# A two-layer encoder with 32 experts per layer: sums kept in PSUM, the gather reading x, one more weight buffer

## The chip, the cores and the metric

The kernel runs on one core of one Trainium2 chip. The metric is the device time of one execution in microseconds. It is written in Bass: every engine has its own instruction list, and semaphores tie them together.

## The reference, cut to what matters

Two layers on x of 256 tokens by 1024 floats, all fp32. The part that the change touches is the second half of a layer:

```
h = rms_norm(x, norm2_g)
g = h @ w_rg + b_rg ; grp = argmax(g)            # 4 groups
e = h @ w_re + b_re, within grp                  # 8 experts a group
gate = softmax(g)[grp] * softmax(top2(e))
for each token and each of its 2 experts:
    y = (silu(h @ w_gate[e]) * (h @ w_up[e])) @ w_down[e]     # 1024 -> 512 -> 1024
    x += gate * y
```

Before it stands the mixer half: a projection by w_in (1024 x 2304), three kinds of attention, a projection by w_out. All 32 experts' weights, 6 MB each, are read in every layer.

## The kernel before

**Staging.** Weights flow through pieces of 1 MB (128 partitions by 2048 floats). Sixteen form the ring; six more, `beside`, are lent by arrays that are idle during the experts: two and the early one in `work`, `tables`, `biased`, `hT`. `ring_plan` (lines 102 to 140) walks through all weights of both layers in the order of use and gives each the piece that comes free first, and with it the semaphore count that SyncE waits for before it issues the load (`piece_in`, line 447). `BESIDE_FREE` says at which count each lent piece is free. Items 8 to 10 use the ring alone, as the next mixers need the arrays. `HALVED` names three pieces a layer that are loaded as two halves, the first half already at half a round (`p_half`). All loads go through SyncE's one queue, in order.

**Items.** The experts are done in 11 items a layer. Items hold 1, 2 or 4 experts, with 128, 64 or 32 token places each, side by side in the 128 columns of TensorE (in order of time 2, 2, 4, 1, 4, 1, 4, 2, 4, 4, 4 experts). An item is: the choice (`pick`, a 0/1 matrix of tokens by places, and `pickw`, the same times the gate weight), built on VectorE from seat numbers (`picks`, line 1714; for item 0 line 1699); the gather, TensorE products with `pick` as the moving operand and the normalised rows as the stationary one (`gathers`, line 948), copied to `xg` by VectorE and ScalarE with the gain of the norm; six rounds (`round_of`, line 978: gate0, gate1, up0, up1, down0, down1, each over one piece of every expert of the item); the transposes of `pickw` (line 1039) and of `hid` (line 1057, read with a step of 4 floats); and `back` (line 1012), four products that scatter y to the tokens. VectorE then adds the four banks to x (line 1750) in each item. The gather of item i+1 is done inside item i, its lower half after round 3 and its upper half after the transposes of `hid`.

**Banks.** Of the eight PSUM banks, 0 and 1 take the gather, 2 the gate product, 3 the up product, 4 and 5 the transposes, 6 and 7 the down product, and 2 to 5 the four products of `back`, so TensorE waits for VectorE's additions (`v_back`) before it writes to 2 to 5 again.

**The normalised rows.** `normed_rows` (line 1207) on ScalarE writes x times the norm's factor into `h`, regrouped so that each block of 128 columns is contiguous; the source is read with a step of 8 floats. The squares before it (line 1125) use `h` as a place to dump.

**The last item** of a layer has matmuls without use between its rounds (`warm`), the turning of the next layer's gains and biases, and its down product in parts, so that little is left behind the last landing.

**Reruns** handle an expert that has more tokens than places. No instruction of that part is in the trace.

## Time and profile before

| what | value |
|---|---|
| median of 3 runs | 1176.21 us (1175.89 to 1178.5) |
| the profiled execution | 1178.81 us, its span 1177.0 us |
| TensorE matmul busy | 997.6 us (85%) |
| VectorE busy | 327.1 us (28%) |
| ScalarE busy | 170.9 us (15%) |
| DMA | 436.80 MB, mean 371 GB/s over the span |
| mean granted TensorE clock | 0.939 |

Busy shares are means over very different stages: the mixers run from the start to about 144 us and from about 585 to 727 us, the experts fill the rest. Matmuls are pipelined, so a busy TensorE is not one at its peak. The DMA share is that of the core's 16 DMA engines; at 1.0 they have no gap.

### The profile page before, as it was taken

The page shows a single profiled execution, that of the slowest core. Times are in us where ns is not written, and L with a number is a line of the kernel's source. Part 1 is how long each engine was busy: PE and PEld are TensorE (multiplying, and loading weights), DVE is VectorE, ACT ScalarE, POOL GpSimd, SP SyncE. Part 2 cuts the span into 40 slices and gives each one's busy share as a digit, 9 for nine tenths or more (in the row PEclk, how much of TensorE's full clock was granted, in tenths as well). Part 3 has the DMA queues.
Part 4 walks back from the last instruction along what each step waited for, and adds up shares of the span by engine and source line. Part 5 has one row for each costly group of instructions (what it writes and reads, how often), then busy time and mean ns, then how long its engine had stood idle before and what let it go on. Part 6 is the DMA issues. An engine that isn't in the chain of part 4 may idle for free.

```text
span 1177.0 us, 14082 instructions
## 1 busy us (share of the span) xinstructions
PE 997.6 (85%) x5406; PEld 467.7 (40%) x5406; DVE 327.1 (28%) x742; ACT 170.9 (15%) x440; POOL 51.6 (4%) x104
## 2 busy tenths in 40 slices
PE   8999999998977946659899999999969779474686
PEld 5556644353423412114356656444424234131242
DVE  3546543221211200102145555432212112010111
ACT  1344311110000100000014333111100001000000
POOL 2121100000000000000021211000000000000000
PEclk9999999999998987878999999999999989788899
DMA  9863889999999999999998247999999999999997
GB/s 307 331 250 114 351 305 416 421 421 420 422 422 420 420 422 356 420 422 421 406 399 305 104 178 286 357 417 420 421 421 422 420 421 421 422 420 422 421 421 281
DMA packets 78132, 436.80 MB, mean 371 GB/s; under 512 B 12800, under 2 KB 15792, under 8 KB 30704
## 3 DMA queue, kind: packets, MB, share of 16 engines
q1 hardware_dynamic: 78064, 435.87, 91.6%
q8 instruction: 45, 0.74, 0.2%
q14 instruction: 23, 0.19, 0.0%
HBM read 434.79 MB, written 1.05 MB: 370 GB/s over the span
## 4 chain that ended last, share of the span: by engine, by line
PE 57%; DMA 31%; SPq 7%; DVE 2%; issue 1%; POOL 1%; DVEq 0%; ACT 0%; POOLq 0%
PE bank L989 27%; DMA ring<-in_w_up 12%; DMA ring<-in_w_down 11%; PE bank L713 9%; PE bank L951 5%; SPq L453 5%; PE bank L840 5%; PE bank L1015 4%; DMA ring<-in_w_gate 2%; DMA biased<-in_w_down 2%; DMA tables<-in_w_down 2%; DMA ring<-in_w_in 1%; SPq L476 1%; PE bank L786 1%; PE bank L776 1%
## 5 line engine op out<-in xcount | busy, mean ns | idle before, releaser
L989 PE MATMUL bank<-ring,work 128*32 128x512 f32 (+2 forms) x2592 | 483.4, 671 | 153.3 <-DMA ring<-in_w_up 59.8
L989 PEld LDWEIGHTS bank<-ring,work 128*32 128x32 f32 (+2 forms) x2592 | 145.3, 131 | 427.9 <-issue 425.9
L713 PE MATMUL bank<-ring,hT 128*128 128x512 f32 (+1 forms) x384 | 128.3, 488 | 2.4 <-DMA ring<-in_w_in 1.2
L951 PE MATMUL bank<-work,h 128*128 128x128 f32 x704 | 89.9, 284 | 6.6 <-DVE work L1716 5.1
L951 PEld LDWEIGHTS bank<-work,h 128*128 128x128 f32 x704 | 85.2, 198 | 21.9 <-issue 15.2
L713 PEld LDWEIGHTS bank<-ring,hT 128*128 128x128 f32 x384 | 71.3, 190 | 49.9 <-issue 42.2
L1746 DVE COPY work<-bank 128x512 f32<-128x512 f32 x22 | 15.2, 691 | 253.6 <-PE bank L989 251.2
L1015 PE MATMUL bank<-work 128*128 128x512 f32 x176 | 81.4, 604 | 2.4 <-ACT work L1294 1.6
L1736 DVE TENSOR_TENSOR work<-work,bank 128x512 f32<-128x512 f32 x22 | 15.1, 687 | 238.4 <-PE bank L989 238.4
L1750 DVE TENSOR_TENSOR x<-x,bank 128x512 f32<-128x512 f32 x88 | 60.5, 687 | 44.3 <-PE bank L1015 44.3
L840 PE MATMUL bank<-ring,h 128*128 128x512 f32 x128 | 58.2, 600 | 0.0
L989 PE MATMUL bank<-work 128*32 128x512 f32 (+2 forms) x176 | 57.5, 594 | 0.0
L1289 ACT COPY work<-bank 128x512 f32<-128x512 f32 x22 | 12.9, 585 | 273.9 <-PE bank L1057 273.9
L1015 PEld LDWEIGHTS bank<-work 128*128 128x128 f32 x176 | 31.8, 190 | 50.9 <-issue 49.2
L1283 ACT COPY work<-bank 128x256 f32<-128x256 f32 x22 | 8.2, 372 | 299.3 <-PE bank L1039 299.3
L1715 DVE TENSOR_TENSOR work<-iota,work 128x512 f32<-128x512 f32 x20 | 13.8, 692 | 126.4 <-PE bank L1039 125.1
L989 PE MATMUL bank<-biased,work 128*32 128x512 f32 (+1 forms) x80 | 40.6, 655 | 0.0
L1294 ACT COPY work<-bank 128x512 f32<-128x512 f32 x22 | 12.9, 585 | 177.2 <-PE bank L989 159.9
L674 PE MATMUL bank<-ident 128*128 128x384 f32 x94 | 36.2, 531 | 2.8 <-DMA ident<-in_c_ident 2.8
L989 PE MATMUL bank<-hT,work 128*32 128x512 f32 (+1 forms) x80 | 36.3, 597 | 0.0
L989 PE MATMUL bank<-tables,work 128*32 128x512 f32 (+2 forms) x80 | 36.1, 594 | 0.0
L1272 ACT ACTIVATE work<-bank,gain 128x128 f32<-128x128 f32 x88 | 25.1, 368 | 57.9 <-PE bank L951 57.9
(206 smaller groups left out, 708.8 us busy)
## 6 DMA issues: line engine op xcount, KB each, us to landing
ring<-in_w_gate SPq DMA_DIRECT2D x110, 1024.0 KB, 26.0
ring<-in_w_up SPq DMA_DIRECT2D x108, 1024.0 KB, 26.7
ring<-in_w_down SPq DMA_DIRECT2D x100, 1024.0 KB, 26.5
ring<-in_w_in SPq DMA_DIRECT2D x10, 1536.0 KB, 14.8
work<-in_w_up SPq DMA_DIRECT2D x10, 1024.0 KB, 10.3
ring<-in_w_out SPq DMA_DIRECT2D x8, 1024.0 KB, 16.9
work<-in_w_gate SPq DMA_DIRECT2D x8, 1024.0 KB, 17.2
ring<-in_w_down SPq DMA_DIRECT2D x16, 512.0 KB, 12.1
```

Of the source, the lines that this page charges most:

```text
L453: sp.dma_start(rows(pos, k), w[:, 0, half * k:half * k + k]).then_inc(landed[pos], 16)
L674: matmul(bank[b][:, 0:3 * P].rearrange("p (n s) -> p n s", n=3), ident[:], ident[:].unsqueeze(1).broadcast_to([P, 3, P]), start=True, stop ...
L713: last = matmul(bank[6 + i % 2][:, 0:c1 - c0], hT[:, k, t * P:t * P + P], group_in(l, gi)[:, k, c0:c1], start=(k == 0), stop=(k == KD - 1))
L840: last = matmul(bank[6 + n % 2][:, :], mixed[:, pos0 + c, t * P:t * P + P], rows(pos, 2)[:, c % 2, half * 512:half * 512 + 512], start=(c ...
L951: last = nc.tensor.matmul(bank[k // 4][:, k % 4 * P:k % 4 * P + P], h_kc[:, t, k, :], pick[:, t, :], start=(t == 0), stop=(t == TT - 1))
L989: last = nc.tensor.matmul(bank[b][e * w:e * w + w, :], lhs[:, k, e * w:e * w + w], rows(pos, k_count // 2)[:, kk, n * 512:n * 512 + 512], ...
L1015: last = nc.tensor.matmul(bank[2 + n][:, :], pickT[:, t, :], y[:, half * 512:half * 512 + 512], start=True, stop=True)
L1272: last = nc.scalar.mul(xg[:, k, :], bank[1][:, (k - 4) * P:(k - 3) * P], gain2[:, q // NI, k:k + 1])
L1715: seated(tt(hot, over(iota[:, 0:P], 1, 2 * TT), wide(seats[:, TIME[i], :], P), ALU.is_equal))
L1736: tt(hid, hid, bank[3][:, :], ALU.mult).then_inc(v_hid, 1)
L1746: nc.vector.tensor_copy(y[:, 512:1024], bank[7][:, :]).then_inc(v_y, 1)
L1750: tt(xs, xs, bank[2 + n][:, :], ALU.add).then_inc(v_back[n], 1)
```

## The change

- `h` becomes a seventh lent piece. Its count is `a_ms`, the fourth square of the layer; the early piece moves from index 21 to 22. The halved pieces are now the second of item 1's last round and the first two of item 2's first.
- `normed_rows` is gone. The gather reads x itself as its stationary operand (`x_kc`, a step of 8 floats), and the norm's factor `rstd` goes into `pick`: each column block is built by a tensor-scalar operation (is equal, then times), four for item 0, eight for each other item, for pick and pickw alike.
- The four products of `back` accumulate in banks 2 to 5 over the 11 items of a layer (start in item 0, stop in item 10), and VectorE adds them to x once, in the last item. Everything else of an item lives in two of the banks 0, 1, 6 and 7 (`pair`), which alternate from item to item; the waits follow from that. The transposes of `pickw` go to the other pair. In the last item they come before the warming matmuls and the next layer's gains and biases, and waits for `a_pickT` and `a_silu` are added.

```diff
@@ -67,7 +67,7 @@
 
 PIECE = 2048
 PIECES = 16
-BESIDE = 6
+BESIDE = 7
 AGAIN = 16
...
@@ -89,14 +89,14 @@
 
 
 
-BESIDE_FREE = [("p_pv", 8, 24)] * 4 + [("p_logit", 2, 40), ("p_pv", 8, 24)]
-TABLES, BIASES, TURNED_ROWS, EARLY = PIECES + 2, PIECES + 3, PIECES + 4, PIECES + 5
+BESIDE_FREE = [("p_pv", 8, 24)] * 4 + [("p_logit", 2, 40), ("a_ms", 4, 41), ("p_pv", 8, 24)]
+TABLES, BIASES, TURNED_ROWS, EARLY = PIECES + 2, PIECES + 3, PIECES + 4, PIECES + 6
 
 BESIDE_LAST = 7
 
 
 
-HALVED = {(l, *key): 2 * l + n for l in range(LAYERS) for key, n in (((1, 5, 0), 1), ((1, 5, 1), 2), ((2, 0, 0), 2))}
+HALVED = {(l, *key): 2 * l + n for l in range(LAYERS) for key, n in (((1, 5, 1), 1), ((2, 0, 0), 2), ((2, 0, 1), 2))}
 
 
 def ring_plan():
...
@@ -217,7 +217,7 @@
         mixed = h[:].rearrange("p (c s) -> p c s", c=KD)
         qk_b = h[:, D:2 * D].rearrange("p (t c) -> p t c", t=TT)
 
-        h_kc = h[:].rearrange("p (t k c) -> p t k c", t=TT, k=KD)
+        x_kc = x[:].rearrange("p t (c k) -> p t k c", k=KD)
 
 
         prob = [proj[:, :, c:c + 512].rearrange("p b (m s) -> p b m s", m=2) for c in (SEG0["C"], SEG0["B"])]
...
@@ -246,7 +246,7 @@
         windows = [s[0:GRID, P:P + 3 * n + 250] for s, n in zip(staged, head_step)]
         gain_rows = [s[0:3 * KD, P + 3 * n + 250:2 * P + 3 * n + 250] for s, n in zip(staged, head_step)]
 
-        beside = [work[:, 0:PIECE], work[:, PIECE:2 * PIECE], tables[:], biased[:], hT_flat, work[:, 2 * PIECE:3 * PIECE]]
+        beside = [work[:, 0:PIECE], work[:, PIECE:2 * PIECE], tables[:], biased[:], hT_flat, h[:], work[:, 2 * PIECE:3 * PIECE]]
         o = [2 * PIECE]
 
         def carve(n):
...
@@ -358,6 +359,11 @@
 
 
         BACK = [(0, 0), (1, 0), (0, 1), (1, 1)]
+
+        SUM0 = 2
+
+        def pair(i):
+            return ((6, 7), (0, 1))[i % 2]
 
         def quad_queries(n):
             g, h0, _ = QUADS[n]
...
@@ -548,9 +554,9 @@
                         if (l, i, r, e) in HALVED:
                             half_in(l, i, r, e, ids[e], 0)
 
-                            if i == 2:
-                                half_in(l, 1, 5, 1, bass.ds(STATIC[3], 1), 1)
-                            if (i, e) != (1, 1):
+                            if (i, e) == (2, 1):
+                                half_in(l, i, r, 0, ids[0], 1)
+                            if (i, e) != (2, 0):
                                 half_in(l, i, r, e, ids[e], 1)
                         elif r < 5 or i < NI - 1:
                             piece_in(l, i, r, e, ids[e])
...
@@ -945,35 +951,41 @@
                     if c != 0:
                         last.then_inc(p_rank, 1)
 
-            def gathers(done, lo=0, hi=KD):
+            def gathers(done, banks, lo=0, hi=KD):
                 for k in range(lo, hi):
                     for t in range(TT):
-                        last = nc.tensor.matmul(bank[k // 4][:, k % 4 * P:k % 4 * P + P], h_kc[:, t, k, :], pick[:, t, :],
+                        last = nc.tensor.matmul(bank[banks[k // 4]][:, k % 4 * P:k % 4 * P + P], x_kc[:, t, k, :], pick[:, t, :],
                                                 start=(t == 0), stop=(t == TT - 1))
                     if k % 4 == 3:
                         last.then_inc(done, 1)
 
-            def gather_low(q):
+            def gather_low(i, q):
                 pe.wait_ge(v_pick, q + 1)
-                need(pe, v_xg, q)
-                gathers(p_gather, 0, KD // 2)
-
-            def gather_high(q):
-                need(pe, a_xg, q)
-                gathers(p_gather, KD // 2, KD)
-
-            def gather(q):
-                gather_low(q)
-                gather_high(q)
+                if i >= 2:
+                    pe.wait_ge(a_y, q - 1)
+                gathers(p_gather, pair(i), 0, KD // 2)
+
+            def gather_high(i, q):
+                if i >= 2:
+                    pe.wait_ge(v_y, q - 1)
+                if i:
+
+                    pe.wait_ge(a_pickT, q)
+                gathers(p_gather, pair(i), KD // 2, KD)
+
+            def gather(i, q):
+                gather_low(i, q)
+                gather_high(i, q)
 
             def first(l):
-                pe.wait_ge(a_h, TT * (l + 1))
-                gather(l * NI)
+                gather(0, l * NI)
 
             hidc = hid.rearrange("p (f c) -> p c f", c=KE)
 
             def item(l, i, q):
                 n_e, w = KINDS[TIME[i]], PLACE[TIME[i]]
+                b0, b1 = pair(i)
+                other = pair(i + 1)
 
                 def round_of(r, banks, lhs, done):
...
@@ -1012,58 +1024,55 @@
                 def back(ns):
                     for n in ns:
                         t, half = BACK[n]
-                        last = nc.tensor.matmul(bank[2 + n][:, :], pickT[:, t, :], y[:, half * 512:half * 512 + 512],
-                                                start=True, stop=True)
+                        last = nc.tensor.matmul(bank[SUM0 + n][:, :], pickT[:, t, :], y[:, half * 512:half * 512 + 512],
+                                                start=(i == 0), stop=(i == NI - 1))
                         last.then_inc(p_back, 1)
 
                 if i == NI - 1:
-                    gather(q)
+                    gather(i, q)
                 pe.wait_ge(v_xg, q + 1)
-                need(pe, v_back[0], q)
-                round_of(0, (2,), xg, p_round)
+                round_of(0, (b0,), xg, p_round)
                 if i == NI - 1:
-                    warm(7, 5)
+                    warm(other[0], 5)
                 pe.wait_ge(a_xg, q + 1)
-                round_of(1, (2,), xg, p_round)
+                round_of(1, (b0,), xg, p_round)
+                pe.wait_ge(v_pickw, q + 1)
+
+                need(pe, v_y, q)
+                for t in range(TT):
+                    last = nc.tensor.transpose(bank[other[1]][:, t * P:t * P + P], pickw[:, t, :], ident[:])
+                last.then_inc(p_pickT, 1)
                 if i == NI - 1:
-                    warm(7, 5)
+                    warm(b1, 5)
                 if i == NI - 1 and l < LAYERS - 1:
-                    gains_turned(l + 1, 1)
-                    for hd in range(2):
-                        if hd == 1:
-                            pe.wait_ge(v_gains, l + 2)
-                        biases(l + 1, hd, hd)
-                need(pe, v_back[3], q)
-                pe.wait_ge(v_pickw, q + 1)
-                for t in range(TT):
-                    last = nc.tensor.transpose(bank[5][:, t * P:t * P + P], pickw[:, t, :], ident[:])
-                last.then_inc(p_pickT, 1)
-                need(pe, v_back[1], q)
-                round_of(2, (3,), xg, p_round)
+                    gains_turned(l + 1, other[0])
+                    pe.wait_ge(a_pickT, q + 1)
+                    biases(l + 1, 0, other[1])
+                    pe.wait_ge(v_gains, l + 2)
+                    biases(l + 1, 1, other[0])
+                round_of(2, (b1,), xg, p_round)
                 if i == NI - 1:
-                    warm(7, 5)
-                round_of(3, (3,), xg, p_round)
+                    pe.wait_ge(a_silu, q + 1)
+                    warm(b0, 5)
+                round_of(3, (b1,), xg, p_round)
                 if i == NI - 1:
-                    warm(7, 4)
+                    warm(b0, 4)
                 if i < NI - 2:
-                    gather_low(q + 1)
+                    gather_low(i + 1, q + 1)
                 elif i == NI - 1 and l < LAYERS - 1:
                     for hd in range(2, 4):
                         pe.wait_ge(v_rel, 4 * l + 4 + hd - 1)
-                        biases(l + 1, hd, hd - 2)
+                        biases(l + 1, hd, other[3 - hd])
                 pe.wait_ge(v_hid, q + 1)
-                need(pe, v_back[2], q)
                 for c in range(KE):
-                    last = nc.tensor.transpose(bank[4][:, c * P:c * P + P], hidc[:, c, :], ident[:])
+                    last = nc.tensor.transpose(bank[b0][:, c * P:c * P + P], hidc[:, c, :], ident[:])
                 last.then_inc(p_hidT, 1)
                 if i < NI - 2:
-                    gather_high(q + 1)
+                    gather_high(i + 1, q + 1)
                 pe.wait_ge(a_hidT, q + 1)
-                need(pe, a_y, q)
-                need(pe, v_y, q)
-                round_of(4, (6, 7), hidT, p_round)
+                round_of(4, (b0, b1), hidT, p_round)
                 if i < NI - 1:
-                    round_of(5, (6, 7), hidT, p_down)
+                    round_of(5, (b0, b1), hidT, p_down)
                 else:
                     lower_rows(0, (0, 1))
                 pe.wait_ge(a_pickT, q + 1)
...
@@ -1203,10 +1212,6 @@
                 mean_squares(t, 2 + t)
                 act.wait_ge(p_yT, 4 * l + 2 * t + 2)
                 copy(hT[:, 4:8, t * P:t * P + P], bank[2 * t + 1][:, :].rearrange("p (k s) -> p k s", k=4)).then_inc(a_yT, 1)
-
-            def normed_rows(l, t):
-                act.wait_ge(g_rstd, rooted(l, "y0" if t == 0 else "y1"))
-                nc.scalar.mul(h_kc[:, t], x[:, t].rearrange("p (c k) -> p k c", k=KD), rstd[:, 2 + t:3 + t]).then_inc(a_h, 1)
 
             def mixers(l):
                 if l == 0:
...
@@ -1681,12 +1682,11 @@
                 link(nc.vector.tensor_reduce(over_n, over_yes, AX_X, ALU.add))
                 nc.vector.tensor_copy(again[:, AGAIN:AGAIN + 1], over_n[0:1]).then_inc(v_flags, 1)
 
-            def copy_gathered(q):
+            def copy_gathered(i, q):
                 dve.wait_ge(p_gather, 2 * q + 1)
-                tt(xg[:, 0:4, :], bank[0][:, :].rearrange("p (k s) -> p k s", k=4), wide(gain2[:, q // NI, 0:4], P), ALU.mult).then_inc(v_xg, 1)
-
-            pair_hot = pick.rearrange("p t (e s) -> p (t e) s", e=2)
-            pair_hotw = pickw.rearrange("p t (e s) -> p (t e) s", e=2)
+                tt(xg[:, 0:4, :], bank[pair(i)[0]][:, :].rearrange("p (k s) -> p k s", k=4), wide(gain2[:, q // NI, 0:4], P), ALU.mult).then_inc(v_xg, 1)
+
+            half_of = [slice(e * P // 2, (e + 1) * P // 2) for e in range(2)]
 
             def first(l):
                 q = l * NI
...
@@ -1696,70 +1696,86 @@
 
                 seated(stt(rgc[:, 0:TT], bank[5][:, 0:2 * NE].rearrange("p (t n) -> p t n", t=TT)[:, :, e0:e0 + 2], 1.0,
                            chosen[:, :, e0:e0 + 2], ALU.add, ALU.mult))
-                tt(pair_hot, over(iota[:, 1:P // 2 + 1], 1, 2 * TT), wide(rgc[:, 0:TT, :].rearrange("p t e -> p (t e)"), P // 2),
-                   ALU.is_equal).then_inc(v_pick, 1)
+                for t in range(TT):
+                    for e in range(2):
+                        last = ts(pick[:, t, half_of[e]], iota[:, 1:P // 2 + 1], rgc[:, t, e:e + 1], rstd[:, 2 + t:3 + t],
+                                  ALU.is_equal, ALU.mult)
+                last.then_inc(v_pick, 1)
                 expert_order(l)
                 placings(l)
                 expert_order_rest(l)
-                copy_gathered(q)
+                copy_gathered(0, q)
                 gates(l)
                 seated(nc.vector.tensor_copy(rgc[:, TT:], rg[:, TT:, e0:e0 + 2]))
-                dve.wait_ge(v_pick, q + 1)
                 dve.wait_ge(p_round, 5 * q + 1)
-                tt(pair_hotw, pair_hot, wide(rgc[:, TT:, :].rearrange("p t e -> p (t e)"), P // 2), ALU.mult).then_inc(v_pickw, 1)
+                for t in range(TT):
+                    for e in range(2):
+                        last = ts(pickw[:, t, half_of[e]], iota[:, 1:P // 2 + 1], rgc[:, t, e:e + 1], rgc[:, TT + t, e:e + 1],
+                                  ALU.is_equal, ALU.mult)
+                last.then_inc(v_pickw, 1)
                 seatings(l)
 
             weights = col[:, 10:12, :].rearrange("p c t -> p (c t)")
 
+            def seats_marked(i, factors):
+
+                for n in range(2 * TT):
+                    last = ts(hot[:, n], iota[:, 0:P], seats[:, TIME[i], n:n + 1], factors[n], ALU.is_equal, ALU.mult)
+                seated(last)
+
             def picks(i, q):
-                seated(tt(hot, over(iota[:, 0:P], 1, 2 * TT), wide(seats[:, TIME[i], :], P), ALU.is_equal))
+                seats_marked(i, [rstd[:, 2 + n % TT:3 + n % TT] for n in range(2 * TT)])
                 tt(pick, hot[:, 0:TT], hot[:, TT:], ALU.add).then_inc(v_pick, 1)
                 dve.wait_ge(v_pick, q + 1)
-                seated(tt(hot, hot, wide(weights, P), ALU.mult))
+                seats_marked(i, [weights[:, n:n + 1] for n in range(2 * TT)])
                 tt(pickw, hot[:, 0:TT], hot[:, TT:], ALU.add).then_inc(v_pickw, 1)
 
             def item(l, i, q):
+                b0, b1 = pair(i)
+                other = pair(i + 1)
                 if i == NI - 1:
                     picks(i, q)
-                    copy_gathered(q)
+                    copy_gathered(i, q)
                 if i < NI - 2:
                     dve.wait_ge(p_pickT, q + 1)
                     picks(i + 1, q + 1)
                     if i == 1:
                         list_again(l)
                 if i == NI - 1 and l < LAYERS - 1:
-                    gains_turned(l + 1, 1)
+                    gains_turned(l + 1, other[0])
                     for hd in range(2):
-                        biases(l + 1, hd, hd)
+                        biases(l + 1, hd, other[1 - hd])
                 dve.wait_ge(a_silu, q + 1)
                 dve.wait_ge(p_round, 5 * q + 4)
-                tt(hid, hid, bank[3][:, :], ALU.mult).then_inc(v_hid, 1)
+                tt(hid, hid, bank[b1][:, :], ALU.mult).then_inc(v_hid, 1)
                 if i < NI - 2:
-                    copy_gathered(q + 1)
+                    copy_gathered(i + 1, q + 1)
                 if i == NI - 1 and l < LAYERS - 1:
                     for hd in range(2, 4):
-                        biases(l + 1, hd, hd - 2)
+                        biases(l + 1, hd, other[3 - hd])
+                if i < NI - 1:
+                    dve.wait_ge(p_down, 2 * q + 2)
+                    nc.vector.tensor_copy(y[:, 512:1024], bank[b1][:, :]).then_inc(v_y, 1)
+                    return
                 for n, (t, half) in enumerate(BACK):
-                    if n == (2 if i == NI - 1 else 0):
+                    if n == 2:
                         dve.wait_ge(p_down, 2 * q + 2)
-                        need(dve, p_back, 4 * q)
-                        nc.vector.tensor_copy(y[:, 512:1024], bank[7][:, :]).then_inc(v_y, 1)
+                        nc.vector.tensor_copy(y[:, 512:1024], bank[b1][:, :]).then_inc(v_y, 1)
                     dve.wait_ge(p_back, 4 * q + n + 1)
-                    need(dve, v_back[n], q)
                     xs = x[:, t, half * 512:half * 512 + 512]
-                    tt(xs, xs, bank[2 + n][:, :], ALU.add).then_inc(v_back[n], 1)
+                    tt(xs, xs, bank[SUM0 + n][:, :], ALU.add).then_inc(v_back[n], 1)
```

Left out: ScalarE's copies, which read the banks of `pair(i)` and `pair(i + 1)` in place of 1, 2, 4, 5 and 6 (same sizes), the counts of `v_back` (now one per layer), the semaphore `a_h`, and the rerun part.

## Rows read from the trace of the kernel before

**Rows 1.** The page's slices: busy tenths of the DMA in 40 slices.
```profile
DMA  9863889999999999999998247999999999999997
```

**Rows 2.** Busy time by stage; columns: engines' busy us, granted clock, DMA share, GB/s.
```profile
160.00:620.00 460.00, 377.17 (x2106) 161.55 (x2103) 90.47 (x162) 39.73 (x94) 7.16 (x16) 0.92 1.02 414
...
736.00:1164.00 428.00, 344.68 (x1996) 143.45 (x1992) 79.75 (x148) 34.76 (x84) 0.00 (x0) 0.92 1.01 416
...
1164.00:1177.00 13.00, 7.72 (x40) 2.27 (x40) 3.44 (x5) 0.58 (x1) 0.00 (x0) 1.00 0.36 137
```

**Rows 3.** The same view, stretches of 2 us.
```profile
144.00:146.00 2.00, 1.30 (x12) 1.33 (x12) 1.76 (x11) 0.19 (x2) 0.00 (x0) 0.97 0.74 307
...
146.00:148.00 2.00, 2.00 (x20) 2.00 (x19) 1.83 (x11) 0.00 (x0) 0.00 (x0) 1.00 0.07 29
...
182.00:184.00 2.00, 2.00 (x12) 0.72 (x10) 0.00 (x0) 0.00 (x0) 0.00 (x0) 1.00 0.94 295
...
730.00:732.00 2.00, 2.00 (x15) 2.00 (x15) 0.84 (x3) 0.00 (x0) 0.00 (x0) 0.70 0.00 0
```

**Rows 4.** Timeline of the sync engine's queue: start, us, issues.
```profile
140.34 0.33 SPq L453 DMA_DIRECT2D hT<-in_w_down  x1
...
150.41 3.76 SPq L465 DMA_DIRECT2D ring<-in_w_down  x3
...
735.07 3.76 SPq L465 DMA_DIRECT2D ring<-in_w_down  x3
```

**Rows 5.** The chain that ended last, from 143 us: start, us, what.
```profile
144.12 0.44 DVE work L1699
...
144.70 3.81 PE bank L951 x32
...
148.50 7.02 PE bank L989 x32
...
155.52 0.37 PE bank L1039 x2
...
167.16 7.02 PE bank L989 x32
...
203.47 3.63 PE bank L1015 x8
...
270.43 26.62 DMA ring<-in_w_down
```

**Rows 6.** Weight loads (min/median/max ns), the chain at two transposes, ScalarE's timeline.
```profile
L1057 PEld LDWEIGHTS bank<-ident,work x88: 195/209/219, 164.6 to 1155.6; 128*128 128x128 f32 x88
...
L1039 PEld LDWEIGHTS bank<-ident,work x44: 137/140/145, 155.5 to 1138.4; 128*128 128x128 f32 x44
...
164.89 0.48 PE bank L1057 x4
...
134.87 1.94 PE bank L848 x16
...
136.26 1.06 ACT L1125 ACTIVATE h<-x 128x1024 f32<-128x1024 f32 x1
...
137.78 4.19 ACT L1209 ACTIVATE h<-x,rstd 128x1024 f32<-128x1024 f32 x2
```

**Rows 7.** VectorE's timeline, and its row of one form of the choice.
```profile
143.23 0.22 DVE L1571 TENSOR_TENSOR work<-work 128x64 f32<-128x64 f32 x1
...
143.37 0.22 DVE L1572 TENSOR_TENSOR work<-work 128x64 f32<-128x64 f32 x1
...
159.45 0.43 DVE L1716 TENSOR_TENSOR work<-work 128x256 f32<-128x256 f32 x1
...
68.66 1.14 DVE L1452 TENSOR_SCALAR work<-work,rden 128x256 f32<-128x256 f32 x4
...
L1715 DVE TENSOR_TENSOR work<-iota,work 128x512 f32<-128x512 f32 x20 | 13.8, 692 | 126.4 <-PE bank L1039 125.1 <-issue 1.2
```

**Rows 8.** The chain at the layers' boundary.
```profile
579.94 17.49 DMA ring<-in_w_in
```

More of the change, by code:

```diff
@@ L300, in encoder @@
         g_fold = sem("g_fold")
-        a_ms, a_sq, a_turn, a_exp, a_pt, a_mixed, a_yT, a_h = (
-            sem("a_" + n) for n in ("ms", "sq", "turn", "exp", "pt", "mixed", "yT", "h"))
+        a_ms, a_sq, a_turn, a_exp, a_pt, a_mixed, a_yT = (
+            sem("a_" + n) for n in ("ms", "sq", "turn", "exp", "pt", "mixed", "yT"))
+        frees["a_ms"] = a_ms
         a_rexp, a_silu, a_pickT, a_xg, a_hidT, a_y = (
@@ L1006, in lower_rows @@
                                 pe.wait_ge(d_last[kk], 16 * n_e * (l + 1))
-                            last = nc.tensor.matmul(bank[6 + half][e * w:e * w + w, :], hidT[:, 2 + kk, e * w:e * w + w],
+                            last = nc.tensor.matmul(bank[(b0, b1)[half]][e * w:e * w + w, :], hidT[:, 2 + kk, e * w:e * w + w],
                                                     rows(pos, 2)[:, kk, half * 512:half * 512 + 512], start=False, stop=(kk == 1))
@@ L1082, in rerun @@
                 pe.wait_ge(r_pick, x0 + 1)
-                gathers(r_gather)
+                gathers(r_gather, (0, 1))
                 pe.wait_ge(r_xg, x0 + 1)
                 pe.wait_ge(d_again, (x0 + 1) * 96)
-                for b, done in ((2, r_gate), (3, r_up)):
+                for b, done in ((6, r_gate), (7, r_up)):
                     for k in range(KD):
-                        last = nc.tensor.matmul(bank[b][:, :], xg[:, k, :], rows(2 * b - 4 + k // 4, 4)[:, k % 4, :],
+                        last = nc.tensor.matmul(bank[b][:, :], xg[:, k, :], rows(2 * b - 12 + k // 4, 4)[:, k % 4, :],
                                                 start=(k == 0), stop=(k == KD - 1))
@@ L1091, in rerun @@
                 for t in range(TT):
-                    last = nc.tensor.transpose(bank[5][:, t * P:t * P + P], pickw[:, t, :], ident[:])
+                    last = nc.tensor.transpose(bank[0][:, t * P:t * P + P], pickw[:, t, :], ident[:])
                 last.then_inc(r_pickT, 1)
@@ L1095, in rerun @@
                 for c in range(KE):
-                    last = nc.tensor.transpose(bank[4][:, c * P:c * P + P], hidc[:, c, :], ident[:])
+                    last = nc.tensor.transpose(bank[1][:, c * P:c * P + P], hidc[:, c, :], ident[:])
                 last.then_inc(r_hidT, 1)
@@ L1106, in rerun @@
                 for n, (t, half) in enumerate(BACK):
-                    last = nc.tensor.matmul(bank[2 + n][:, :], pickT[:, t, :], y[:, half * 512:half * 512 + 512],
-                                            start=True, stop=True)
+                    last = nc.tensor.matmul(bank[SUM0 + n][:, :], pickT[:, t, :], y[:, half * 512:half * 512 + 512],
+                                            start=False, stop=False)
                 last.then_inc(r_back, 1)
@@ L1131, in x_squares @@
                     for half in range(2):
-                        act.wait_ge(v_back[BACK.index((t, half))], l * NI)
+                        act.wait_ge(v_back[BACK.index((t, half))], l)
                 mean_squares(t, t)
@@ L1761, in rerun @@
-                dve.wait_ge(r_step, x0 * 3 + 3)
-                tt(pickw, pick, wide(rgc[:, TT:, 0], P), ALU.mult).then_inc(r_pick, 1)
+                dve.wait_ge(r_step, x0 * 2 + 2)
+                for t in range(TT):
+                    ts(pick[:, t], iota[:, 0:P], rgc[:, t, 1:2], rstd[:, 2 + t:3 + t], ALU.is_equal, ALU.mult)
+                    last = ts(pickw[:, t], iota[:, 0:P], rgc[:, t, 1:2], rgc[:, TT + t, 0:1], ALU.is_equal, ALU.mult)
+                last.then_inc(r_pick, 1)
                 dve.wait_ge(r_gather, x0 * 2 + 2)
@@ L1779, in rerun @@
                 dve.wait_ge(r_done, x0 + 1)
-                for n, (t, half) in enumerate(BACK):
-                    xs = x[:, t, half * 512:half * 512 + 512]
-                    last = tt(xs, xs, bank[2 + n][:, :], ALU.add)
-                last.then_inc(r_done, 1)
+                dve.sem_inc(r_done, 1)
             run_layers(dve, extra, mixers, first, item, rerun, seen[3])
```

43 lines of the change are left out of this document (18 added, 25 removed).

## The prediction

> **What bounds the kernel now.** I read the page's slices first, then busy time by stage, then the stretches where the DMA is not busy, then the sync engine's queue and the chain there, and last the duration of single instructions.
>
> The slices show a kernel that streams weights: the DMA is at 9 tenths or more in all but two troughs, one in each layer's mixers [rows 1]. By stage, the 460 us of the first layer's experts have a DMA share of 1.02 at 414 GB/s, the 428 us of the second's 1.01 at 416 GB/s, while TensorE is busy 377 and 345 us of them [rows 2]. So the experts' time is bytes over bandwidth: a piece of 1024 KB costs 1.049/0.415 = 2.53 us. Only the last 13 us are work behind the last landing [rows 2]. What can be won is (a) DMA time in the troughs, (b) the tail, (c) nothing else: an engine that gets faster inside an expert item gives TensorE more waiting.
>
> The trough has two kinds of idle time. During the mixers every buffer is full and none comes free. At its end the same happens once more: after the sync engine has issued the piece into hT (140.34) its next issue is at 150.41, behind the first half round of item 0; in layer 1 that one is at 735.07 [rows 4]. The DMA drains its queue and stands: share 0.07 at 146 to 148, 0.00 at 730 to 732 [rows 3]. At 144 to 146 it was still at 0.74, so it stops near 145.5 and stands about 4.8 us until 150.41; in layer 1 it stops before 730 and stands at least 5.1 us, until 735.07 [rows 3, 4]. One more free buffer there is filled for nothing.
>
> Behind that stretch TensorE, not the DMA, is the pace for a while. Its chain has no gap from 144.70 to 270.43, where it first waits for a landing, 26.62 us long [rows 5]. A round of item 0 takes 3.5 us (two in 7.02), the transposes of pickw 0.37, gather and transposes between rounds 3 and 4 take 4.25 (148.50 + 7.02 + 0.37 + 7.02 = 162.91, to 167.16), the back matmuls 3.63, an item 29.3 (167.16 + 7.02 = 174.18, to 203.47). Each round of items 0 and 1 frees two pieces (of the first only one is used again): at 152.0 (1), 155.5, 159.4, 162.9, 170.7, 174.2; 29.3 later for item 1: 181.3, 184.8, 188.7, 192.2, 200.0, 203.5; item 2 frees four at 210.6. The DMA wants one per 2.53 us. From 170.7 four pieces last until 180.8, and the next is free at 181.3; from there twelve last until 211.7, and the next four are free at 210.6. So there is no slack until 181 and 1.1 us at 211, and from then on it grows by 4 x 2.53 - 3.5 = 6.6 us a round. The dip of the share to 0.94 at 182 to 184 is such an edge [rows 3]. Whatever makes TensorE later before 211 is paid in DMA time; what makes it later after that is free.
>
> **The change part by part.**
>
> *The 23rd piece.* h becomes a buffer, free once the square of the second routed half has been taken (a_ms 4). That square starts at 136.26 and takes 1.06 us [rows 6], before the wait that stands ahead of it in the sync queue is met at 140.34 [rows 4], so the new piece is issued right behind the one into hT and the DMA runs on for 2.53 us where it stood 4.8 (layer 1: 5.1 or more). It fits wholly in both. The frees behind it are the same ones at the same times, each now taken by the piece after the one that took it before (the halved pieces move along by one too, and wait for the same half rounds), so the DMA keeps the piece it is ahead. In the stretch at DMA pace it then has 1 MB less to move: -2.53 us a layer, -5.05 in all. The boundary passes it on: layer 1's first projection is released by the landing of w_in, 17.49 us after its issue, out of a full queue [rows 8]; the tail starts from a landing too.
>
> *The gather reads x.* Two ACT copies go, 4.19 us together from 137.78, so until 141.97 [rows 6]; the gather started at 144.70, released by the choice (144.12 + 0.43) [rows 5]. Gain 0. Nothing took cover beside them. The choice for item 0 becomes four tensor-scalar operations of 128x64 in place of one 128x256 of 0.43 us. Nearest rows: two independent 128x64 operations start 0.14 apart and take 0.22, which gives 3 x 0.14 + 0.22 = 0.64; four 128x256 tensor-scalars take 1.14, so 0.285 for four times the columns each, which at best makes four small ones as long as now [rows 7]. Bounds 0 to +0.45 (four wholly serial, 0.22 each), I take +0.2 a layer, and it counts, since the gather is on the path: +0.4. In the items the choice is eight operations of 128x128 for two of 0.69 [rows 7]; by 1.14/8 = 0.14 to 0.28 each that is 1.1 to 2.3 us for 1.4. In item 0, where it comes latest, it is ready at 159.45 + 0.43 = 159.88 [rows 7], 3.0 us before the gather at 162.9; so 0, and if that cover went, at most 0.8 an item.
>
> *The stationary operand of the gather.* The weight load now reads x with a step of 8 floats, 32 bytes. No row before has that on TensorE. From below: hid is turned with a step of 16 bytes, its loads take 209 ns against 140 for contiguous ones, but four pairs pass in 0.48 us, 120 ns each, as contiguous x does (16 in 1.94, 121 ns): loads are hidden in the matmul before [rows 6]. A gather of 32 pairs in 3.81 is 119 ns each [rows 5], so +0 (a gain is excluded: contiguous is the best case). From above: ACT reads x at exactly this step in 4.19/2 = 2.10 us for 1024 elements, against 1.06 contiguous, 2.05 ns an element [rows 6]; 128 of them are 262 ns, which a matmul of 119 ns doesn't cover: +143 ns x 32 = +4.6 us a gather. I take 0, the row of the same engine; the other end is the first rival.
>
> The Trainium skill speaks against this edit: "SBUF — State Buffer", section "Door 1: The DMA port swizzle", gives 16-byte lines, wants two hits a line and calls 4 fp32 the widest free step; 8 is beyond it. Both rows fit it (hid at 4 keeps the pace, ACT at 8 halves), and by it the sum would be the first rival's and not -4.65.
>
> *Sums in four banks.* 20 of 22 items lose their four DVE additions of 128x512 (0.69 us each by the row of that size [rows 7], 2.8 an item) and the waits for them. TensorE has no gap there in the chain until 270 [rows 5], and after it waits for landings: 0. New waits, for the copies of y of two items back and of the turned weights, are met a round or more before. The last item keeps its additions, so the tail's 13 us stay [rows 2]. Where a last item's TensorE waits for the new a_pickT and a_silu, warming matmuls stand between, and the full DMA queue covers them [rows 8]: 0.
>
> **Sum**: -5.05 + 0.4 = -4.65. The profiled execution took 1178.81 (span 1177.0) and gives 1174.2; the median of the runs, 1176.21, is 2.6 lower, and gives **1171.6 us**. Own range 1170.6 (the choice at no cost, a piece at 2.6 us) to 1173.0 (choice at its upper bound, 5 ns more a pair).
>
> **Rivals.**
>
> *1. The strided load shows.* With g more per gather, item 0's start is late by g, its round 4 by 2g, item 1's by 3g; the fourth falls past 211, where slack is. Per layer 3g - 1.1 (2g where that is more) against 2.53 won. For: the ACT row, and the longer load of hid. Against: hid's pace. If the ratio 209/140 fell on the pair's pitch, 119 to 178 ns, g = 1.9 and the kernel takes 2 x (5.7 - 1.1 - 2.53) + 0.4 = +4.5: 1180.7. With ACT's rate g = 4.6: 2 x (13.8 - 1.1 - 2.53) + 0.4 = +20.7: 1196.9. It decides from 3g - 1.1 = 2.33, g = 1.14 us, a pair at 155 ns. This is the case slower than before.
>
> *2. The piece is hidden anyway.* The DMA ends the tight stretch no earlier, since TensorE's frees set it (to 211) and the piece it is ahead is lost when items 8 to 10 fall back to the 16 of the ring: 1176.2 + 0.4 = 1176.6, no gain. For: the tight stretch. Against: frees are passed on one to one, and TensorE waits 26.62 us at 270 [rows 5].
>
> *3. One layer's worth only*, because h is free late or the sync queue stands before it: 1176.2 - 2.53 + 0.4 = 1174.1. Against: the square of layer 1 is the same work at the same place.
>
> **How the numbers follow.** Forecast 0.57; rival 1 0.27 (half of it below 1188); rival 2 0.09; rival 3 0.07. A measurement of this kernel can't tell less than 0.2%, 2.4 us, so 1173.9 to 1178.6 is no change. Faster: the forecast and a little of rival 3, 0.59. Same: rival 2, the rest of 3 and a mild rival 1, 0.16. Slower 0.25. The range runs from 1169.8 to 1188, which leaves out some 0.15 above (the full ACT rate) and 0.03 below.
>
> **What would show it.** A DMA issue into h right behind the one into hT, and the share at 146 to 148 near 1. The gather still 3.8 us for 32 pairs and its loads near 209 ns or not much over; over 300 ns with a pair above 155 is rival 1, with a share below 1 between 170 and 211 as its mark. The stretches at DMA pace 2.5 us shorter each, TensorE's first wait for a landing no shorter than before. Wrong overall: a time above 1174 with a gather of 3.8 us, or a time below 1169, which no term here gives.

## The result, and the profile after

The changed kernel takes 1193.18 us, the median of 4 runs (1191.64 to 1193.9), against 1176.53 of the kernel before measured beside it (1175.89 to 1178.5): a ratio of 1.0134, 95% interval 1.0118 to 1.015. I had forecast 1171.6 with a range up to 1188; the first rival, with ScalarE's price, was 1196.9.

The page's view of instruction groups, changed kernel (busy us, mean ns of one, then idle before it). L957 is the gather, L1068 the transposes of hid, L1723 the choice in the items, L1701 that of item 0, L1766 the additions to x.

```profile
L957 PE MATMUL bank<-work,x 128*128 128x128 f32 x704 | 175.1, 405 | 2.6 <-DVE work L1701 2.6
L957 PEld LDWEIGHTS bank<-work,x 128*128 128x128 f32 x704 | 171.1, 334 | 16.8 <-issue 12.5 <-DVE work L1701 2.8 <-DVE work L1728 0.9
...
L1723 DVE TENSOR_SCALAR work<-iota,work,rstd 128x128 f32<-128x128 f32 x80 | 22.3, 343 | 177.2 <-PE bank L1043 175.5 <-issue 1.6
...
L1068 PEld LDWEIGHTS bank<-ident,work 128*128 128x128 f32 x88 | 14.5, 226 | 4.4 <-DVE work L1750 3.6 <-issue 0.6
...
L1766 DVE TENSOR_TENSOR x<-x,bank 128x512 f32<-128x512 f32 x8 | 5.5, 689 | 27.0 <-PE bank L1027 27.0
...
L1701 DVE TENSOR_SCALAR work<-iota,rgc,rstd 128x64 f32<-128x64 f32 x8 | 2.0, 311 | 0.1
```

The same two groups of the kernel before (its line 951):

```profile
L951 PE MATMUL bank<-work,h 128*128 128x128 f32 x704 | 89.9, 284 | 6.6 <-DVE work L1716 5.1
L951 PEld LDWEIGHTS bank<-work,h 128*128 128x128 f32 x704 | 85.2, 198 | 21.9 <-issue 15.2
```

The additions fell from 88 to 8 as forecast. The gather's weight loads now take 334 ns in the mean, in place of 198, and its matmuls hold TensorE for 175.1 us, in place of 89.9. The chain of the changed kernel (start, us, what), which answers to [rows 5]:

```profile
143.15 0.99 DVE work L1701 x4
144.15 0.04 issue
144.19 7.91 PE bank L957 x32
152.10 7.02 PE bank L1001 x32
159.12 0.37 PE bank L1043 x2
159.49 7.02 PE bank L1001 x32
166.51 4.00 PE bank L957 x16
170.51 0.47 PE bank L1068 x4
170.98 3.80 PE bank L957 x16
174.78 7.02 PE bank L1001 x32
181.79 3.63 PE bank L1027 x8
```

The first gather takes 7.91 us instead of 3.81, a later one 4.00 + 3.80: 247 and 244 ns a pair. Everything else of an item is what it was, to 0.01 us. The choice of item 0 takes 0.99 us, not 0.44. Item 0's round 4 starts at 174.78 in place of 167.16, although this execution had begun its choice 0.97 us earlier (143.15 for 144.12).

The sync engine's queue: the new piece goes out where it should (the line with h), but the wait behind it ends at 154.01 in place of 150.41 [rows 4].

```profile
139.52 0.33 SPq L459 DMA_DIRECT2D hT<-in_w_down  x1
139.89 0.43 SPq L459 DMA_DIRECT2D h<-in_w_down  x1
154.01 2.04 SPq L471 DMA_DIRECT2D ring<-in_w_down  x2
...
733.30 0.43 SPq L459 DMA_DIRECT2D h<-in_w_down  x1
```

And what the DMA makes of it, in busy time by stretch (the last two columns are its share and GB/s):

```profile
146.00:148.00 2.00, 2.00 (x10) 2.00 (x9) 0.68 (x5) 0.00 (x0) 0.00 (x0) 0.50 0.60 250
148.00:150.00 2.00, 2.00 (x10) 2.00 (x10) 1.42 (x6) 0.00 (x0) 0.00 (x0) 0.91 0.02 8
176.00:178.00 2.00, 2.00 (x12) 0.72 (x10) 0.00 (x0) 0.01 (x1) 0.00 (x0) 1.00 0.21 86
178.00:180.00 2.00, 2.00 (x12) 0.67 (x10) 0.00 (x0) 0.00 (x0) 0.00 (x0) 1.00 0.37 53
210.00:212.00 2.00, 2.00 (x12) 0.63 (x10) 0.00 (x0) 0.00 (x0) 0.00 (x0) 1.00 0.34 139
212.00:214.00 2.00, 2.00 (x12) 0.66 (x10) 0.00 (x0) 0.56 (x1) 0.00 (x0) 1.00 0.53 115
```

The kernel before in three of these stretches:

```profile
176.00:178.00 2.00, 2.00 (x7) 0.69 (x7) 1.54 (x3) 0.00 (x0) 0.00 (x0) 1.00 1.00 422
178.00:180.00 2.00, 2.00 (x12) 0.64 (x10) 0.53 (x1) 0.00 (x0) 0.00 (x0) 1.00 1.01 426
210.00:212.00 2.00, 2.00 (x24) 0.65 (x20) 0.00 (x0) 0.00 (x0) 0.00 (x0) 1.00 1.03 430
```

At 146 to 148 the piece in h fills time that was empty (share 0.60 for 0.07 [rows 3]). Then the DMA stands from 148 on, and two holes are new, at 176 to 180 and 210 to 214: one behind each of the two gathers inside items 0 and 1, where the walk of the frees had little slack or none. Layer 1 has such holes too (shares 0.12 at 770 to 772 and 0.11 at 804 to 806).

### The profile page after: what moved, and what is told of

Same layout as the page of the kernel before. It is cut to its first block, busy times and chain, and to the rows that moved or that the text cites. A ratio compares the mean times of both kernels' runs of the same rounds, so it can differ in the third digit from the quotient of the medians.

```text
span 1192.1 us, 13918 instructions
## 1 busy us (share of the span) xinstructions
PE 1068.3 (90%) x5406; PEld 551.0 (46%) x5406; DVE 291.6 (24%) x794; ACT 162.8 (14%) x436; POOL 51.6 (4%) x104
## 4 chain that ended last, share of the span: by engine, by line
PE 68%; DMA 22%; SPq 6%; DVE 2%; issue 1%; POOL 1%; ACT 0%; DVEq 0%; POOLq 0%
PE bank L1001 29%; PE bank L957 12%; DMA ring<-in_w_up 9%; PE bank L719 9%; DMA ring<-in_w_down 8%; PE bank L1027 5%; PE bank L846 5%; SPq L459 4%; DMA ring<-in_w_gate 2%; PE bank L680 2%; DMA ring<-in_w_in 1%; SPq L482 1%; PE bank L792 1%; PE bank L782 1%; PE bank L814 1%
## 5 line engine op out<-in xcount | busy, mean ns | idle before, releaser
L1001 PE MATMUL bank<-ring,work 128*32 128x512 f32 (+2 forms) x2512 | 463.2, 651 | 93.3 <-DMA ring<-in_w_up 40.1
L1001 PEld LDWEIGHTS bank<-ring,work 128*32 128x32 f32 (+2 forms) x2512 | 139.1, 127 | 357.8 <-issue 352.7
L957 PEld LDWEIGHTS bank<-work,x 128*128 128x128 f32 x704 | 171.1, 334 | 16.8 <-issue 12.5
L957 PE MATMUL bank<-work,x 128*128 128x128 f32 x704 | 175.1, 405 | 2.6 <-DVE work L1701 2.6
L1001 PE MATMUL bank<-work 128*32 128x512 f32 (+2 forms) x176 | 68.3, 614 | 8.8 <-DMA ring<-in_w_down 8.8
L1723 DVE TENSOR_SCALAR work<-iota,work,rstd 128x128 f32<-128x128 f32 x80 | 22.3, 343 | 177.2 <-PE bank L1043 175.5
L1290 ACT COPY work<-bank 128x512 f32<-128x512 f32 x22 | 12.9, 586 | 293.0 <-PE bank L1068 293.0
L1001 PE MATMUL bank<-biased,work 128*32 128x512 f32 (+1 forms) x80 | 36.2, 595 | 0.0
L1001 PE MATMUL bank<-h,work 128*32 128x512 f32 (+1 forms) x80 | 36.1, 594 | 0.0
L846 PEld LDWEIGHTS bank<-ring,h 128*128 128x128 f32 x128 | 23.2, 190 | 25.2 <-issue 25.0
```

Source lines behind the costliest of these rows:

```text
L846: last = matmul(bank[6 + n % 2][:, :], mixed[:, pos0 + c, t * P:t * P + P], rows(pos, 2)[:, c % 2, half * 512:half * 512 + 512], start=(c ...
L957: last = nc.tensor.matmul(bank[banks[k // 4]][:, k % 4 * P:k % 4 * P + P], x_kc[:, t, k, :], pick[:, t, :], start=(t == 0), stop=(t == TT ...
L1001: last = nc.tensor.matmul(bank[b][e * w:e * w + w, :], lhs[:, k, e * w:e * w + w], rows(pos, k_count // 2)[:, kk, n * 512:n * 512 + 512], ...
L1290: nc.scalar.copy(hidT.rearrange("p c s -> p (c s)"), bank[b0][:, :]).then_inc(a_hidT, 1)
L1723: last = ts(hot[:, n], iota[:, 0:P], seats[:, TIME[i], n:n + 1], factors[n], ALU.is_equal, ALU.mult)
```

## The experiments

Eleven kernels ran, in three groups, each group beside runs of the kernel before.

**step8_alone.** The kernel before, and only the step of 8 floats moved from ScalarE's read of x to TensorE's read of h. (Dots in a diff mark what is left out between two places.)

```diff
-        h_kc = h[:].rearrange("p (t k c) -> p t k c", t=TT, k=KD)
+        h_kc = h[:].rearrange("p (t c k) -> p t k c", t=TT, k=KD)
...
-                nc.scalar.mul(h_kc[:, t], x[:, t].rearrange("p (c k) -> p k c", k=KD), rstd[:, 2 + t:3 + t])
+                nc.scalar.mul(h[:, t * D:t * D + D], x[:, t], rstd[:, 2 + t:3 + t])
```

> The kernel before, with one thing moved: ScalarE writes the normalised rows to h without regrouping them, and TensorE's weight load of the gather reads h with the step of 8 floats. Banks, choice, additions and the 22 pieces stay. If the step is the cause (in the changed kernel a pair of the gather passes in 7.91/32 = 247 ns against 119, g = 4.1 us), each layer loses 3g - 1.1 = 11.2 us of DMA time: 1176.5 + 22.4 = 1199, gathers at 247 ns a pair. If instead the two-bank items, the choice or the lent h slow the changed kernel, this one takes 1176 to 1177.

1196.18 us, ratio 1.0162 (1.0141 to 1.0182). Its weight loads and its first gather, from one line's view and the chain:

```profile
L951 PEld LDWEIGHTS bank<-work,h x704: 312/335/338, 144.0 to 1146.6; 128*128 128x128 f32 x176
...
144.04 7.86 PE bank L951 x32
```

The step alone costs more than the whole loss of the change. The time is 3 us below my figure of 1199; the trace of grouped_all, below, suggests why.

**grouped_all and grouped_none.** The changed kernel with 22 pieces and a regrouped copy of x in h. The one gathers from the copy in all items, the other from x in all, with nothing else between them.

```diff
+                for t in range(TT):
+                    act.wait_ge(a_ms, 4 * l + 3 + t)
+                    nc.scalar.mul(h_kc[:, t], x[:, t].rearrange("p (c k) -> p k c", k=KD), one[:]).then_inc(a_h, 1)
...
-            def gathers(done, banks, lo=0, hi=KD):
+            def gathers(done, banks, lo=0, hi=KD, i=None):
+                rows_of = h_kc if i in GROUPED else x_kc
```

> The changed kernel with 22 pieces and the regrouped copy (ScalarE copies x to h in blocks of 128 contiguous columns, no factor), so the gather's weight load is contiguous; sums in four banks, alternating pairs and the factor in the choice stay. By the step theory only the choice is left to pay, measured 0.99 against 0.44 us before the first gather: 1176.5 + 1.1 = 1177.6. By the rival (the banks' new waits, or the eight small operations of a choice, cost the time) it stays at or above 1190.

> The kernel grouped_all, and only the gather's operand changed back to x with a step of 8 floats. By the step theory 1177.6 + 22.4 = 1200; seen from the changed kernel, which has one piece more a layer, 1193.2 + 5.0 = 1198. If the step costs nothing it equals grouped_all. If it is over 5 us above the changed kernel, the 23rd piece is worth more than its 2.53 us a layer.

1178.89 us (ratio 1.001, 0.9998 to 1.0022) and 1196.99 us (1.0171, 1.015 to 1.0192). So sums in four banks, alternating pairs and the longer choice together cost at most 0.2%, and the step costs 18.1 us. The chain at the first gather, first of grouped_all, then of grouped_none:

```profile
143.76 5.44 PE bank L961 x32
```

```profile
143.97 7.88 PE bank L961 x32
```

The profiled grouped_all ran part of its first gather at a granted clock of 0.50, the lower of the two levels, and took 5.44 us for it in both layers, as layer 1 of the kernel before did; at a clock of 1.00 the same gather takes 3.81. The strided one takes 7.88 us in grouped_none, with the clock at 0.50 from 144 to 150, and 7.86 in step8_alone, with the clock at 1.00 throughout. So the first gather loses 2.4 or 4.1 us, by the state of the clock. This is an account after the fact, from one trace of each kernel: with 2.4 + 4.0 + 4.0 - 1.1 = 9.3 us a layer the sum is 18.6, for 18.1 measured. It also fits the spread of the runs: those of grouped_all lie within 4.9 us, those of grouped_none within 1.6.

**grouped_early and grouped_late.** The same kernel, `GROUPED = (0, 1, 2)` and `GROUPED = range(3, NI)`: the step only in the gathers of items 3 to 10, and only in those of items 0 to 2.

> The kernel grouped_all, with the gathers of items 3 to 10 reading x with the step of 8 floats and those of items 0, 1 and 2 the regrouped copy. By the walk of the frees only the first three gathers are paid: as grouped_all, 1178.9, within 1.5 us, though TensorE is busy 14 of 22 gathers x 4 us = 60 us more. If every gather is paid, 16/22 of the 18.1 us between grouped_all and grouped_none: 1192.

> The mirror of it: the gathers of items 0, 1 and 2 read x with the step of 8 floats, those of items 3 to 10 the regrouped copy. By the walk of the frees it pays the whole: 1197, as grouped_none. If every gather is paid alike, 6/22 of 18.1 us: 1184.

1178.11 us (1.0007, 0.9994 to 1.0019) and 1196.96 us (1.0162, 1.0147 to 1.0178). Three gathers a layer carry the whole price, the other eight none that the runs can tell. Busy time by stage of grouped_early:

```profile
160.00:620.00 460.00, 406.02 (x2106) 192.14 (x2103) 72.67 (x182) 39.80 (x94) 8.74 (x17) 0.94 1.02 414
...
736.00:1164.00 428.00, 378.73 (x2008) 175.54 (x2002) 61.08 (x171) 34.73 (x84) 0.00 (x0) 0.93 1.01 416
```

TensorE is busy 406 and 379 us there, 63 us more than in [rows 2], and the DMA still has no hole: share and rate are those of before.

**step4, step2, step1.** The changed kernel with another layout of the rows of w_gate and w_up over the partitions, which makes the gather's step 4, 2 or 1 floats. The price of a smaller step is the DMA's contiguous run: 8, 4 and 2 KB a partition, where it was 8. The diff is shortened; in the kernels the numbers stand in place of B.

```diff
-                w = a[name][l:l + 1, e].rearrange("l e (p k) c -> p (l e) k c", k=k)
+                w = a[name][l:l + 1, e].rearrange("l e (a p b) c -> p (l e) a b c", a=8 // B, b=B)   # B = 4, 2, 1; not w_down
...
-        x_kc = x[:].rearrange("p t (c k) -> p t k c", k=KD)
+        x_abc = x[:].rearrange("p t (a c b) -> p t a b c", a=8 // B, b=B)
```

> The changed kernel, with the rows of w_gate and w_up laid out as (2 halves, 128 partitions, 4 rows) in place of (128 partitions, 8 rows): each piece is still 8 KB contiguous a partition, and the gather reads x with a step of 4 floats, 16 bytes. If that step is free as it was for the transposes of hid (120 ns a pair), the gather falls to about 3.8 to 3.9 us and the forecast of the change comes true but for the choice: 1176.5 - 5.05 + 1.1 = 1172.6. If any step beyond one line's second hit costs as ScalarE's row does, the gather stays at 7.9 us and the time at 1193. Between: a pair at 178 ns, g = 1.9, 2 x (4.6 - 2.53) + 1.1 = 1181.8.

> The changed kernel with the rows of w_gate and w_up laid out as (4 blocks, 128 partitions, 2 rows): each descriptor reads 4 KB, and the gather reads x with a step of 2 floats, 8 bytes, so two reads fall in each 16 bytes. At steps of 8 and 4 floats a pair took 247 and 242 ns. If the cost comes with the first read that finds no second one in its 16 bytes, the gather is back at 3.8 us and the time at 1177 - 5.05 + 1.1 = 1173, up to 1176 where TensorE's clock is low in the first gather. If any step but 1 costs, the gather stays near 7.8 us and the time at 1191. If descriptors of 4 KB cost DMA rate (the rate below 416 GB/s at a share of 1.0), it is above 1180 with a short gather.

> The same with (8 blocks, 128 partitions, 1 row): the gather reads x contiguously, in any theory at 3.8 us, and each descriptor of w_gate and w_up reads 2 KB. Without a cost of the small descriptors the time is 1177 - 5.05 + 1.1 = 1173, up to 1176 where the clock is low. With one, the share of the DMA stays at 1.0 and the rate falls: 2% of rate on two thirds of the bytes would be +12 us.

1190.85 us (1.0115, 1.0095 to 1.0135), 1192.07 (1.0116, 1.01 to 1.0131) and 1220.77 (1.0365, 1.0351 to 1.0379). None is a gain, for two different reasons. The weight loads (min/median/max ns) and the chain at the first gather inside an item, step4:

```profile
L970 PEld LDWEIGHTS bank<-work,x x704: 307/330/332, 144.4 to 1137.8; 128*128 128x128 f32 x176
...
166.57 3.93 PE bank L970 x16
170.50 0.47 PE bank L1081 x4
```

step2:

```profile
L970 PEld LDWEIGHTS bank<-work,x x704: 193/196/336, 145.3 to 1135.9; 128*128 128x128 f32 x176
...
164.99 2.08 PE bank L970 x16
```

step1:

```profile
L970 PEld LDWEIGHTS bank<-work,x x704: 186/192/337, 143.9 to 1159.5; 128*128 128x128 f32 x176
...
163.75 1.98 PE bank L970 x16
```

A step of 16 bytes costs an ordinary weight load as much as 32 (330 and 335 ns; 7.73 and 7.91 us for the 32 pairs of the first gather, so 242 and 247 ns each); 8 bytes costs 0.1 us in 16 pairs (2.08 + 1.89 us for 32, so 124 ns each). In the same kernel the transposes of hid, with the same 16 bytes, pass four in 0.47 us. And the rate of the DMA in the experts of layer 0, step2 first, then step1:

```profile
160.00:620.00 460.00, 372.19 (x2092) 159.85 (x2089) 69.58 (x182) 37.69 (x91) 5.15 (x13) 0.91 1.02 405
```

```profile
160.00:620.00 460.00, 360.40 (x2044) 150.12 (x2041) 63.27 (x163) 36.66 (x88) 1.48 (x4) 0.91 1.04 393
```

The DMA is as full as before, at 405 and 393 GB/s for 414 [rows 2]; in layer 1 it is 404 and 392 for 416. An estimate by layer 0's rates: 2.2% and 5.1% of some 890 us at DMA pace are 20 and 45 us, and the runs are 19 and 47 above the 1173 to 1174 that a contiguous gather with 23 pieces gives (below).

**swap_norm and swap_norm_22.** A contiguous gather and the 23rd piece together. h keeps the normalised, regrouped rows as before, and x itself is lent: no one reads it between the routing and the last item. In the last item x is formed again from h, which VectorE reads there with a step of 128 floats (x and the bank are contiguous; my expectation, which speaks of a step of 8, is wrong in this). The diff is shortened.

```diff
-BESIDE_FREE = [("p_pv", 8, 24)] * 4 + [("p_logit", 2, 40), ("a_ms", 4, 41), ("p_pv", 8, 24)]
+BESIDE_FREE = [("p_pv", 8, 24)] * 4 + [("p_logit", 2, 40), ("a_h", 2, 41), ("p_pv", 8, 24)]
...
-        beside = [..., hT_flat, h[:], work[:, 2 * PIECE:3 * PIECE]]
+        beside = [..., hT_flat, x[:].rearrange("p t d -> p (t d)"), work[:, 2 * PIECE:3 * PIECE]]
...
+                seated(nc.vector.reciprocal(inv[:], rstd[:, 2:4]))
...
-                    tt(xs, xs, bank[SUM0 + n][:, :], ALU.add).then_inc(v_back[n], 1)
+                    stt(xs, old, inv[:, t:t + 1], bank[SUM0 + n][:, :].rearrange("p (c k) -> p c k", k=KD), ALU.mult, ALU.add)
```

The choice is that of the kernel before. swap_norm_22 is the same with the 22 pieces of before.

> A version with both: contiguous gather and 23 pieces. ScalarE writes the normalised rows regrouped to h, as in the kernel before, the gather and the 0/1 choice are as before, the sums stay in four banks, and the buffer of x itself is lent as the 23rd piece, since nobody reads x until the last item; there VectorE forms x again as h divided by the norm's factor plus the bank, with a step of 8 floats. If the step was all that ate the piece's gain: 1177.2 - 2 x 2.5 + up to 1.4 for the strided addition at each layer's end = 1172 to 1174. If the piece is worth nothing by itself (hidden anyway): 1177 or more.

> The same kernel with 22 pieces, x not lent. The difference to swap_norm is the worth of one piece a layer alone: 5.0 us if it is two pieces' DMA time, 0 if it is hidden. Against the kernel before it has only the sums in four banks and the strided addition: 1177 to 1178.5.

1172.94 us (ratio 0.996, 0.9945 to 0.9976) and 1179.42 us (1.001, 0.9996 to 1.0023). The piece alone is worth 6.5 us between these medians. Their runs spread by 5.4 and 8.0 us, and a first gather at the low clock costs 1.63 us a layer (5.44 for 3.81), which may be part of that spread; so the 5.05 of the sum agrees with it. swap_norm_22 lies 0.9 us above what I had expected, within that spread. From the chain and the groups of swap_norm: the gathers at full speed, and the addition in the last item, with its strided read of h, at 1.11 us in place of 0.69.

```profile
143.89 3.81 PE bank L963 x32
...
162.10 1.98 PE bank L963 x16
...
L1769 DVE SCALAR_TENSOR_TENSOR x<-h,inv,bank 128x512 f32<-128x512 f32 x8 | 8.5, 1109 | 24.9 <-PE bank L1034 24.9
```

**swap_norm_warm.** `warm(7, 3)` becomes `warm(7, 3 + 2 * l)`.

> swap_norm with five in place of three warming matmuls before the routing of layer 1 is done. In the kernel before, the first gather of layer 1 took 5.44 us against 3.81 in layer 0 at half the clock, after 4.8 us of idle TensorE. If the two more keep the clock up, 1.6 us less than swap_norm; if they end behind the choice, up to 1 us more; else the same.

1174.23 us (0.9968, 0.9955 to 0.9981), not told apart from swap_norm. In its trace the first gather of layer 1 took 3.81 us, but so did swap_norm's; the half clock comes and goes between executions (in swap_norm_warm it was layer 0 that had 5.44). Inconclusive.

## Why the prediction was wrong

**The step that failed** is the one on the stationary operand: "I take 0, the row of the same engine". The price is g = 4.0 to 4.1 us a gather, 0.5 short of the upper end that I had worked out from ScalarE's row (247 ns a pair; that row gave 262). I had given the whole first rival 0.27 and left this end of it, some 0.15, outside my range; the measured time lies there. All marks named for that rival came: loads over 300 ns, a pair above 155, and a DMA share below 1 between 170 and 211. The row that I chose was of the same engine but of another operation. The transposes of hid are loaded in another way than an ordinary fp32 operand: contiguous, 140 ns against 192 in the gather of the kernel before; at a step of 4 floats, 209 against 330 (step4). The first of these differences stood in the trace of the kernel before, in a row that I had not put beside the others (min/median/max ns), and should have told me that the row of hid did not answer the question:

```profile
L951 PEld LDWEIGHTS bank<-work,h x704: 186/192/334, 144.7 to 1124.2; 128*128 128x128 f32 x176
```

The runs show the difference; what in the engine makes it, they don't. Nor do they show that ScalarE's figure lay so near for one common reason: VectorE, reading h with a step of 128 floats, took 1.5 times as long, not twice.

**The rule that I set aside** was the better guide. The Trainium skill, "SBUF — State Buffer", section "Door 1: The DMA port swizzle", wants two hits in each 16-byte line. Step 2 has them and keeps 196 ns, steps 4 and 8 have one and pay 330 and 335: the runs agree. Its sentence that fp32 may step by 4 for free does not hold for these loads (242 ns a pair in step4), and the measurement decides. I had read the two as one rule; at a step of 4 they part, and the row of hid, which kept its pace there, could not speak for the first. My words "by it the sum would be the first rival's" were right, and I did not let them move the forecast.

**The walk of the frees held.** "Whatever makes TensorE later before 211 is paid in DMA time; what makes it later after that is free" is grouped_late (+19.4 us over the kernel before) and grouped_early (+0.5). Rival 1's formula with the measured g of 4.1 gives 2 x (12.3 - 1.1 - 2.53) + 0.4 = +17.7; measured +16.65. That the changed kernel's loss came so near is in part luck: the formula leaves out the clock in the first gather and has the choice too small.

**The 23rd piece** did what was forecast, and where: issued right behind the piece into hT (at 139.89, and at 733.30 in layer 1), for -5.05 by the sum, and measured at -6.5 between swap_norm and swap_norm_22 and at -3.8 between the changed kernel and grouped_none. It was not hidden anyway, so rival 2 falls. Rival 3, one layer's worth of 2.53, lies below both measured figures, and its reason, a piece that is late in one layer, is not in the trace.

**The choice** was mis-sized: +0.55 a layer by 0.99 against 0.44, above my upper bound of +0.45. A 128x64 tensor-scalar with two scalars a partition takes 311 ns and starts 0.23 after the one before, not 0.14; of the neighbours that I took, one had no such scalars, the other one scalar and four times the columns. Worth 1.1 us in all, under what a run can tell. The lower end of my own range was also wrong by its own terms: the choice at no cost and a piece at 2.6 us give 1171.0, not 1170.6.

**The sums in four banks** cost and bring nothing: grouped_all and swap_norm_22 both lie at 1.001, with 1 inside the interval. 55 us less of VectorE's work (80 additions of 0.69) were off the path, as forecast.

So +16.65 is, to within 0.7 us, the step at 18.1, the rest of the edits at 1.7 (which no run tells from nothing), and the piece at -3.8.

## What to carry to other kernels

A bound from a neighbouring row is only as good as the likeness of the operation: compare first how the two kinds stand where both are measured (192 against 140 ns contiguous), and when a written rule, a second engine's row and half of the chosen row (the longer load) all point one way, put the forecast there or split it. In a kernel that streams through a fixed number of buffers, walk the frees against the transfer rate: here three gathers of eleven carried all of the cost, and the eight later ones were each slowed by 4 us for nothing (grouped_early). And when a buffer is wanted, look for the array that is not read, rather than making a reader take a worse layout: lending x in place of h gave both, 0.4% faster than the kernel before.

## What the runs showed of the hardware

- An ordinary fp32 weight load of 128x128 takes 192 ns contiguous, 196 at a step of 2 floats, 330 at 4, 335 at 8; a pair of load and matmul of 128 columns passes in 119, 124, 242 and 247 ns. A transposing load takes 140 ns contiguous and 209 at a step of 4 floats, and its pair passes in some 120 ns either way.
- Where the granted clock is at 0.50 in a part of a gather of 32 pairs, the contiguous one takes 5.44 us for 3.81 (grouped_all, swap_norm), the strided one 7.88 for 7.86 (grouped_none, step8_alone).
- With contiguous runs of 8, 4 and 2 KB a partition in two thirds of the bytes, the full DMA moves 414, 405 and 393 GB/s.
- VectorE's scalar_tensor_tensor of 128x512, with one operand in a PSUM bank: 1.11 us where the other one is read with a step of 128 floats (swap_norm, line 1769), 0.75 where it is contiguous (the same kernel, line 1484): 1.5 times. ScalarE, at a step of 8 floats, took twice as long [rows 6].
